# An encoder block with a 32-expert mixture on one core: a ring of eleven weight slots in place of ten, with a gather that reads the tokens themselves

## The chip, the core and the metric

The kernel runs on one core of one Trainium2 chip. The metric is device time in microseconds (us), smaller is better. The engines named below are TensorE (PE, with its weight loads PEld), VectorE (DVE), ScalarE (ACT), GpSimd (POOL) and SyncE (SP, which here issues nearly all transfers).

## The reference

One layer over 256 tokens of width 1024, all in 4-byte floats. Cut to what matters:

```
h = x
h = h + mixer(rmsnorm(h))                   # in-projection, dilated attention and MLA, out-projection
h = h + cross_attention(rmsnorm(h), rmsnorm(mem))   # 4 heads, 256 memory tokens
xt = rmsnorm(h) * g_moe                     # (256, 1024)
top_val, top_idx = top_k(xt @ w_router + b_router, 4)       # of 32 experts
gates = softmax(top_val)
for each expert e, for the tokens routed to it:
    gate, up = split(xt[tok] @ w_gate_up[e] + b_gate_up[e])  # (1024 x 2048)
    gate, up = min(gate, 7), clip(up, -7, 7)
    y[tok] += gates * (((up + 1) * gate * sigmoid(1.702 * gate)) @ w_down[e] + b_down[e])
return rmsnorm(h + y) * g_final
```

Each expert has 8 MB of gate-up weights and 4 MB of down weights, 384 MB in all.

## The kernel before

**Stages.** The in-projection z runs first (L1115: for each of eight row blocks k of `w_in`, eight matmuls into eight banks). Then come the attention parts, the cross-attention, its out-projection (`memory_out`, L1387), the router (L1400), the ranks of the tokens within their experts (L1419 to L1424), and the expert loop. The order on every engine is written out by hand. Semaphores join the engines.

**Items.** An expert's tokens are worked in blocks of 64. A block is an *item*; an expert with more than 64 tokens has two or more. An item is on PE: the biases (L1451), gate-up (`item`, L1467, 32 matmuls that the profile counts as 64), the gather of the *next* item's tokens (L1432), the scatter of the *previous* item's output into banks 4 to 7 (L1441), four transposes of the hidden rows (L1479), down (L1487, 16 matmuls, 32 in the profile), and two transposes of the scatter matrix (L1493). DVE clamps gate and up (L1070, L1071), joins them (L1074, L1077) and copies the gathered columns to `xgT` with the gain (`gathered_out`, L989); ACT does the sigmoid (L615) and the copies from PSUM (L618, L622, L624). Gate-up and gathering write two halves of 64 partitions of a bank by turns.

**The gather.** The normalised tokens are split in three bf16 parts (`part`, by `high_part`, `middle_left`, `middle_part`, `low_part` on ACT, DVE and one on POOL at L645), whose sum is the 4-byte value. 48 bf16 matmuls with the one-hot `pick` give the gathered columns.

**The ring.** Expert weights pass through `ring`, NSLOT slots of 2 MB. Expert e is six chunks j = 6e .. 6e+5, four of gate-up and two of down. SP loads chunk j when chunk j - NSLOT has been used by the expert's last item (`chunks_used`). Experts 7 to 26 are loaded in a loop by pairs of chunks (L374, 4 MB, which need two free slots and give notice once); the others one by one (L366). The first ten chunks are loaded ahead as their places come free (`load_chunk`, L327), since the same memory serves the attention parts:

```
            load_chunk(7)
            sp.wait_ge(S["wm_mm"], 4)
            load_chunk(8)
            load_chunk(9)
            sp.wait_ge(S["rt_mm"], 2)
            load_chunk(6)
```

`wm_mm` counts the four groups of `memory_out`, `rt_mm` the two router products.

**The end.** After the last scatter (`y_done`) DVE adds the banks to h (L1083), ACT squares the rows (L628), a small chain gives the scale (L663 to L674), DVE scales the rows (L1090), and SP writes two halves of 512 KB (L400).

Of the kernel before, what the change touches and what calls it, by code (L numbers as in the profile page):

```python
# [28 lines left out]
NSLOT = 10  # L29
REGION = (2, 3, 4, 5, 8, 9, 6, 7, 0, 1)  # L30
LEAD = 2
GROUP = 5
EPS = 1e-6
NORMS = ("x", "mem", "z", "o", "h", "f")
# [12 lines left out]
C_LOGM = C_ID + P  # L47
C_UP = C_LOGM + TT * SEQ
# [9 lines left out]
G_END = 43  # L58


def shape_constants():

    c = np.zeros((P, C_END), np.float32)
    p = np.arange(P)
    c[:, C_ID:C_ID + P] = np.eye(P)
    for t in range(TT):

        off = np.arange(SEQ)[None, :] - (t * P + p)[:, None]
        n = sum(((off % d == 0) & (np.abs(off) <= w // 2)).astype(int) for w, d in PATTERNS)
        c[:, C_LOGM + t * SEQ:C_LOGM + (t + 1) * SEQ] = np.where(n > 0, np.log(np.maximum(n, 1)), -1e30)  # L70
# [7 lines left out]
    return c  # L78


def encoder_kernel(nc, x, xT, mem, pos, pos_col, posk, consts, gains, w_in, w_q_b, w_kv_b, rel_cur, rel_prev, w_o,
# [9 lines left out]
    with ctx:  # L91
# [8 lines left out]
        work = sb("work", 2048 + 4096 + 2048 + 3072 + KC * NE)  # L100
        cst = sb("cst", C_END)
        gain = sb("gain", G_END)
# [9 lines left out]
        def col_area(lo, n):  # L112
            return work[:, lo:lo + n]

        def pair_area(lo, n):
            return work[:, 2048 + lo:2048 + lo + n]

        def turn_area(lo, n):
            return work[:, 6144 + lo:6144 + lo + n]

        def prob_area(lo, n):
            return work[:, 8192 + lo:8192 + lo + n]
# [4 lines left out]
        def slot(j):  # L127
            return region(REGION[j % NSLOT], 0, SLOT)

        def slot_pair(j):  # L130
            return ring[:, REGION[j % NSLOT] * SLOT:(REGION[j % NSLOT] + 2) * SLOT]

        def paired(e):
            return LEAD + GROUP <= e < NE - GROUP

# [13 lines left out]
        win = spl(ring[:, 0:KC * ZW], KC)  # L149
        z = spl(region(0, 0, TT * ZW), TT)  # L150
        bias = region(1, 0, TT * HEADS * SEQ).rearrange("p (t h k) -> p t h k", t=TT, h=HEADS)
        qb = spl(region(2, 0, TT * HEADS * DQB), TT)
        k96 = spl(region(2, 1536, TT * HEADS * DQB), TT)
        v_b = spl(region(2, 3072, TT * WA), TT)
        wmo = spl(ring[:, 0:KC * D], KC)


        def wmkv(k):
            return region((4, 5, 8, 9)[k // 2], k % 2 * 2 * D, 2 * D)
        wo = spl(ring[:, 4 * SLOT:4 * SLOT + KC * D], KC)  # L160
        wmq = spl(ring[:, 8 * SLOT:8 * SLOT + KC * D], KC)


        kT_flat = region(6, 0, KC * SEQ)
        kT_mem = spl(kT_flat, KC)
        v_mem = spl(region(6, 2048, TT * D), TT)
# [3 lines left out]
        wqb = spl(region(7, 0, 2 * HEADS * DQB), 2)  # L170
        wkvb = region(7, 1536, HEADS * (NOPE + DH))
        znT = spl(region(7, 2560, 3 * SEQ), 3)
        rope_t = region(7, 3328, 4 * HEADS * ROPE // 2)
        square_s = spl(region(7, 2560, 2 * SEQ), 2)
        square_sum = spl(region(7, 3072, 2 * SEQ), 2)
        qT_m = spl(region(7, 0, KC * SEQ), KC)
        bgu_raw = region(7, 2048, 2 * D)
# [8 lines left out]
        zero_bf = o_s.bitcast(bf16)  # L186
# [4 lines left out]
        steps = [a.bitcast(bf16).rearrange("p (k q) -> p k q", q=SEQ) for a in (pair_area(0, 4096), region(3, 0, 4096))]  # L191
        qT96 = spl(pair_area(0, HEADS * SEQ), HEADS)
        kT96 = spl(pair_area(2048, HEADS * SEQ), HEADS)
        rest = spl(pair_area(0, TT * D), TT)
        gate_s, up_s, sig_s, h_s = (pair_area(512 * i, 512) for i in range(4))
# [11 lines left out]
        pick = spl(turn_area(1664, TT * BLK // 2).bitcast(bf16), TT)  # L207
# [7 lines left out]
        probT = region(7, 0, 2048).rearrange("p (j g m q) -> p j g m q", j=2, g=2, m=TT)  # L215
# [3 lines left out]
        part = [spl(prob_area(i * D, D).bitcast(bf16), TT) for i in range(3)]  # L219
# [1363 lines left out]
```

## Time and profile before

| what | value |
|---|---|
| median of three runs | 1221.64 us (1220.99 to 1222.2) |
| the profiled execution | 1219.65 us |
| its span, first to last instruction | 1217.8 us |
| PE busy | 1140.9 us (94%) |
| DVE, ACT, POOL busy | 301.4, 199.2, 7.5 us |
| moved by DMA | 440.43 MB, mean 362 GB/s |
| PE share of the chain that ended last | 66%, DMA 19%, DVE 9% |
| items | 33 (L1070 ran 33 times) |

The span begins with the first instruction and ends with the last. The profiled execution takes 1.85 us beyond its span. Busy time says how long an engine had work, not what it cost the whole. The chain that ended last is followed back from the last instruction to what released each step.

### The profile page before, as it was taken

Reading aid. Unit: us, or ns where it says so; the run is one execution under the profiler, and the core shown is the slowest. Engines: PE = TensorE matmul, PEld = TensorE weight load, DVE = VectorE, ACT = ScalarE, POOL = GpSimd, SP = SyncE. Lnnn points to the kernel's source line nnn. Section 1 sums busy time; section 2 is a strip of 40 time slices with the busy share of each in tenths; the row PEclk is TensorE's granted clock in tenths of the full one; section 3 lists DMA queues with packets and bytes.
Section 4 is the critical chain, followed back from the end, with each engine's and each line's share of the span. In section 5 each row is a group of like instructions: output and inputs, shape, how many; then the busy total and the mean of one; then the engine's idle time right before and its main releaser. Section 6 shows DMA issues by size and latency. Waiting matters only on the chain.

```text
span 1217.8 us, 16578 instructions
## 1 busy us (share of the span) xinstructions
PE 1140.9 (94%) x6563; PEld 490.7 (40%) x6563; DVE 301.4 (25%) x683; ACT 199.2 (16%) x375; POOL 7.5 (1%) x13
## 2 busy tenths in 40 slices
PE   7999999998999999999988989889999999999995
PEld 3476555854333333333333333333333333333332
DVE  3366553148212111111211111111111121111113
ACT  2120551223111111111110111111111111111111
POOL 0000010000000000000000000000000000000000
PEclk9999999998999999999999999999999999999998
DMA  9800269326999999999999999999999999999993
GB/s 364 347 1 1 73 275 356 129 100 248 429 426 427 428 428 434 430 429 433 433 431 430 431 430 431 430 429 429 382 430 429 430 432 431 426 427 428 427 427 164
DMA packets 28572, 440.43 MB, mean 362 GB/s; under 512 B 4576, under 2 KB 4704, under 8 KB 10496
## 3 DMA queue, kind: packets, MB, share of 16 engines
q1 hardware_dynamic: 27504, 439.30, 85.3%
q8 instruction: 52, 0.85, 0.3%
q10 hardware_dynamic: 1008, 0.21, 0.1%
q14 instruction: 8, 0.07, 0.0%
HBM read 438.45 MB, written 1.05 MB: 361 GB/s over the span
## 4 chain that ended last, share of the span: by engine, by line
PE 66%; DMA 19%; DVE 9%; ACT 2%; issue 2%; DVEq 2%; SPq 0%; ACTq 0%
PE quad L1467 26%; DMA ring<-in_w_gate_up 19%; PE quad L1487 16%; PE quad L1115 2%; PE bank L1331 2%; PE bank L1115 2%; DVE work L1074 2%; DVE work L1070 2%; PE quad L1479 1%; PE bank L1137 1%; DVE work L1071 1%; ACT work L618 1%; PE bank L1207 1%; PE bank L1278 1%; PE quad L1286 1%
## 5 line engine op out<-in xcount | busy, mean ns | idle before, releaser
L1467 PE MATMUL quad<-ring,work 128*64 128x512 f32 x2112 | 465.8, 598 | 17.0 <-DMA ring<-in_w_gate_up 17.0
L1467 PEld LDWEIGHTS quad<-ring,work 128*64 128x64 f32 x2112 | 148.7, 138 | 315.5 <-issue 283.7
L1487 PE MATMUL quad<-ring,work 128*64 128x512 f32 x1056 | 233.9, 595 | 22.6 <-ACT work L618 22.6
L1487 PEld LDWEIGHTS quad<-ring,work 128*64 128x64 f32 x1056 | 72.8, 137 | 162.5 <-issue 132.0
L1070 DVE TENSOR_SCALAR work<-quad 128x512 f32<-128x512 f32 x33 | 22.8, 691 | 322.3 <-PE quad L1467 322.3
L615 ACT ACTIVATE work<-work 128x512 f32<-128x512 f32 x33 | 20.8, 630 | 464.0 <-DVE work L1070 464.0
L984 DVE CAST work<-cst 96x64 bf16 (+1 forms) x34 | 6.5, 191 | 335.3 <-PE quad L1467 335.3
L1441 PE MATMUL bank<-work 64*128 64x512 f32 x272 | 67.6, 615 | 0.7 <-ACT work L624 0.7
L1432 PEld LDWEIGHTS quad<-work 128*128 128x128 bf16 x1632 | 50.6, 99 | 29.1 <-issue 28.3
L622 ACT ACTIVATE work<-quad 128x512 f32<-128x512 f32 x33 | 19.7, 597 | 237.2 <-PE quad L1487 237.2
L1432 PE MATMUL quad<-work 128*128 128x64 bf16 x1632 | 54.6, 195 | 1.5 <-DVE work L960 1.5
L615 ACT ACT_TABLE_LOAD x33 | 42.3, 1283 | 1.1 <-issue 0.5
L1115 PE MATMUL quad<-ring,work 128*128 128x488 f32 x64 | 29.8, 612 | 8.1 <-DMA ring<-in_w_in 8.1
L618 ACT ACTIVATE work<-quad 128x512 f32<-128x512 f32 x33 | 19.7, 597 | 94.9 <-PE quad L1479 94.9
L979 DVE TENSOR_SCALAR work<-cst,work 128x64 bf16 (+1 forms) x68 | 14.2, 251 | 75.3 <-issue 75.2
L1441 PEld LDWEIGHTS bank<-work 64*128 64x128 f32 x272 | 23.5, 186 | 18.6 <-issue 16.0
L1331 PE MATMUL bank<-work,ring 128*128 128x256 f32 x128 | 27.9, 380 | 1.3 <-DVE work L679 1.3
L1115 PE MATMUL bank<-ring,work 128*128 128x488 f32 x64 | 27.5, 572 | 0.0
L1479 PEld LDWEIGHTS quad<-cst,work 128*128 128x128 f32 x132 | 13.8, 140 | 33.0 <-DVE work L989 33.0
L1479 PE MATMUL quad<-cst,work 128*128 128x128 f32 x132 | 21.7, 286 | 5.7 <-DVE work L989 5.7
L1331 PEld LDWEIGHTS bank<-work,ring 128*128 128x128 f32 x128 | 24.2, 190 | 4.8 <-DVE work L679 1.5
L1074 DVE SCALAR_TENSOR_TENSOR work<-work 128x512 f32<-128x512 f32 x33 | 22.8, 692 | 3.5
(260 smaller groups left out, 772.2 us busy)
## 6 DMA issues: line engine op xcount, KB each, us to landing
ring<-in_w_gate_up SPq DMA_DIRECT2D x40, 4096.0 KB, 35.1
ring<-in_w_gate_up SPq DMA_DIRECT2D x48, 2048.0 KB, 20.4
ring<-in_w_down SPq DMA_DIRECT2D x20, 4096.0 KB, 33.4
ring<-in_w_down SPq DMA_DIRECT2D x24, 2048.0 KB, 21.3
ring<-in_w_mkv SPq DMA_DIRECT2D x8, 1024.0 KB, 23.5
ring<-in_w_in SPq DMA_DIRECT2D x8, 976.0 KB, 16.7
ring<-in_w_o SPq DMA_DIRECT2D x1, 4096.0 KB, 12.9
ring<-in_w_mq SPq DMA_DIRECT2D x1, 4096.0 KB, 22.6
```

Of the source, the lines that this page charges most:

```text
L615: act.activation(sig_s, gate_s, ACT.Sigmoid, scale=ALPHA).then_inc(S["sig_ready"], 1)
L618: act.activation(hT, bank[2][:, :], ACT.Copy).then_inc(S["hid_ready"], 1)
L622: act.activation(o_s, bank[3][:, :], ACT.Copy).then_inc(S["out_copied"], 1)
L1070: dve.tensor_scalar(gate_s, bank[0][:, :], LIMIT, None, ALU.min).then_inc(S["gate_ready"], 1)
L1074: dve.scalar_tensor_tensor(up_s, up_s, 1.0, gate_s, ALU.add, ALU.mult).then_inc(S["gu_ready"], 1)
L1115: ins = mm(bank[4 * t + n][:, 0:ZN], nT[:, k, t * P:(t + 1) * P], win[:, k, n * ZN:(n + 1) * ZN], start=(k == 0), stop=(k == KC - 1))
L1331: ins = mm(bank[4 + c // 2][:, c % 2 * SEQ:(c % 2 + 1) * SEQ], wmq[:, k, c * P:(c + 1) * P], hT_s[:, k, :], start=(k == 0), stop=(k == KC ...
L1432: ins = mm(bank[2][:, c * BLK:(c + 1) * BLK], part[j][:, t, c * P:(c + 1) * P], pick[:, t, :], start=(j == 0 and t == 0), stop=(j == 2 and ...
L1441: ins = mm(bank[4 + 2 * t + n][:, :], gsel[lo:lo + BLK, t * P:(t + 1) * P], o_s[lo:lo + BLK, :], start=False, stop=last, skip_group_check= ...
L1467: ins = mm(bank[n // 2][lo:lo + BLK, :], xgT[:, k * BLK:(k + 1) * BLK], up_rows(j, k)[:, n * 512:(n + 1) * 512], start=False, stop=(k == K ...
L1479: ins = pe.transpose(bank[2][:, c * P:(c + 1) * P], h_s[:, c * P:(c + 1) * P], ident)
L1487: ins = mm(bank[3][n * BLK:(n + 1) * BLK, :], lhs, down_rows(j, f)[:, n * 512:(n + 1) * 512], start=(f == 0), stop=(f == KC - 1))
```

## The change

- The ring has eleven slots. Slot j is region j mod 11; the attention parts move to other regions. To make room, `work` loses its 3072-column score area, which now lies in region 7, and consts and gains shrink. The SP loop is written out; pairs are used for experts 7 to 26 where both chunks lie side by side.
- The chunks loaded ahead are 0 to 10, with other conditions for 6 to 10.
- The gather multiplies the 4-byte tokens h by a 4-byte `pick` that carries the norm's scale: four matmuls to rows of 64 tokens. ACT copies them (`xg_s`), PE transposes them, DVE adds the gain. The bf16 parts are gone on ACT, DVE and POOL.
- Banks 4 to 7 are opened with h (`residual_in`) in place of zeros.
- The last norm reads those banks; the output goes out in four pieces, one of them multiplied by POOL.
- The first loads are small (gains and one column block in one transfer, then half of `w_in`'s first block), and twelve bf16 matmuls on zeros (`warm`) stand ahead of the in-projection. ACT issues its small loads after the first has landed.

```diff
-NSLOT = 10
-REGION = (2, 3, 4, 5, 8, 9, 6, 7, 0, 1)
+NSLOT = 11
+PAIRED = range(7, 27)
...
+        def pair_first(j):
+            return j // NCH in PAIRED and j % 2 == 0 and j % NSLOT < NSLOT - 1
...
+            sp.dma_start(work[:, FRONT - G_END:FRONT + SEQ], xT[:, 0:G_END + SEQ]).then_inc(S["ld_first"], 16)
+            sp.dma_start(win(0, 0, half_row), w_in[0:P, 0:half_row]).then_inc(ld_win[0], 16)
+            sp.dma_start(win(0, half_row, ZW - half_row), w_in[0:P, half_row:ZW]).then_inc(S["ld_half"], 16)
...
             sp.wait_ge(S["bgu_ready"], 1)
+            load_chunk(6)
+            sp.wait_ge(S["om_mm"], MH)
             load_chunk(7)
             sp.wait_ge(S["wm_mm"], 4)
             load_chunk(8)
+            sp.wait_ge(S["wm_mm"], 5)
             load_chunk(9)
             sp.wait_ge(S["rt_mm"], 2)
-            load_chunk(6)
+            load_chunk(10)
...
-            memory_out(3, range(0, 4))
+            memory_out(3, range(0, 4)).then_inc(S["wm_mm"], 1)
...
             def gather():
-                for c in range(KC):
-                    for j in range(3):
-                        for t in range(TT):
-                            ins = mm(bank[2][:, c * BLK:(c + 1) * BLK], part[j][:, t, c * P:(c + 1) * P], pick[:, t, :],
-                                     start=(j == 0 and t == 0), stop=(j == 2 and t == TT - 1))
+                for t in range(TT):
+                    for n in range(2):
+                        ins = mm(bank[2][n * BLK:(n + 1) * BLK, :], pick[:, t, :], h[:, t, n * 512:(n + 1) * 512],
+                                 start=(t == 0), stop=(t == TT - 1))
...
+            def residual_in(t):
+                for n in range(2):
+                    mm(bank[4 + 2 * t + n][:, :], ident, h[:, t, n * 512:(n + 1) * 512], start=True, stop=False,
+                       skip_group_check=True)
...
+            def gathered_columns(w):
+                pe.wait_ge(S["xg_copied"], w + 1)
+                for c in range(4):
+                    ins = pe.transpose(bank[3][:, c * P:(c + 1) * P], xg_s[:, c * P:(c + 1) * P], ident)
+                ins.then_inc(S["xgT_mm"], 1)
...
                 scatter().then_inc(S["scattered"], 1)
-                pe.wait_ge(S["xg_ready"], w + 2)
+                gathered_columns(w + 1)
                 pe.wait_ge(S["hmid_ready"], w + 1)
                 for c in range(4):
                     ins = pe.transpose(bank[2][:, c * P:(c + 1) * P], h_s[:, c * P:(c + 1) * P], ident)
                 ins.then_inc(S["hid_mm"], 1)
                 pe.wait_ge(S["hid_ready"], w + 1)
+                pe.wait_ge(S["xg_ready"], w + 2)
...
+            pe.wait_ge(S["warm_ready"], 1)
+            for i in range(12):
+                mm(bank[7][:, :], warm[:, 0:P], warm[:, :], start=True, stop=True)
...
-            for j in range(4):
-                t, n = divmod(j, 2)
-                dve.tensor_tensor(h[:, t, n * 512:(n + 1) * 512], bank[4 + j][:, :], h[:, t, n * 512:(n + 1) * 512],
-                                  ALU.add).then_inc(S["f_ready"], 1)
+            link(dve.tensor_copy(h[:, 0, 512:D], bank[5][:, :]))
+            link(dve.tensor_tensor_reduce(spare[:, 512:D], h[:, 0, 512:D], bank[5][:, :], 1.0 / D, 0.0, ALU.mult, ALU.add,
+                                          ss[:, 1:2]))
...
+            out_scaled(1, 0)
+            out_scaled(1, 1)
+            out_scaled(0, 0)
```

On PE, one item of the expert loop stood so before (`quad` is banks 0 to 3, `bank` the others; the counts are of matmuls written, two records each in the profile where the operands are 4 bytes wide and not a transpose):

```order
L1451 MATMUL quad<-work 64x512 x4
L1467 MATMUL quad<-ring,work 64x512 x32
L1472 REGISTER_ALU
L1432 MATMUL quad<-work 128x64 x48
L1441 MATMUL bank<-work 128x512 x4
L1479 MATMUL quad<-cst,work 128x128 x4
L1487 MATMUL quad<-ring,work 64x512 x16
L1493 MATMUL quad<-cst,work 128x128 x2
```

And now (`y_banks` is banks 4 to 7):

```order
L1467 MATMUL quad<-work 64x512 x4
L1481 MATMUL quad<-ring,work 64x512 x32
L1486 REGISTER_ALU
L1441 MATMUL quad<-h,work 64x512 x4
L1457 MATMUL y_banks<-work 128x512 x4
L1449 MATMUL quad<-cst,work 128x128 x4
L1493 MATMUL quad<-cst,work 128x128 x4
L1502 MATMUL quad<-ring,work 64x512 x16
L1508 MATMUL quad<-cst,work 128x128 x2
```

The 48 gather matmuls became four, and four transposes (L1449) came in between the scatter and the transposes of the hidden rows.

On PE, between the router's last product and the first item, before:

```order
L1400 MATMUL quad<-work,ring 128x32 x4
L1419 MATMUL quad<-work,up_bf 128x32
L1421 MATMUL quad<-work,ones_bf 128x32
L1422 MATMUL quad<-work,up_bf 128x32
L1423 MATMUL quad<-work,ones_bf 128x32
L1424 MATMUL quad<-work,ones_bf 128x32
L1502 MATMUL bank<-work 128x512 x4
L1432 MATMUL quad<-work 128x64 x48
L1509 MATMUL quad<-cst,work 32x128 x2
```

And now:

```order
L1403 MATMUL quad<-work,ring 128x32 x4
L1423 MATMUL y_banks<-h,cst 128x512 x2
L1429 MATMUL quad<-work,up_bf 128x32
L1431 MATMUL quad<-work,ones_bf 128x32
L1432 MATMUL quad<-work,up_bf 128x32
L1433 MATMUL quad<-work,ones_bf 128x32
L1434 MATMUL quad<-work,ones_bf 128x32
L1423 MATMUL y_banks<-h,cst 128x512 x2
L1441 MATMUL quad<-h,work 64x512 x4
L1519 TENSOR_LOAD work
L1519 ISA x2
L1449 MATMUL quad<-cst,work 128x128 x4
```

The four bf16 matmuls on zeros (L1502) gave way to four 4-byte ones that bring in h (L1423), two ahead of the ranks and two behind; the first gather is followed by a trip over ACT to the transposes at L1449.

## Rows read from the trace of the kernel before

**Rows 1.** The page: the span, and what DMA moved in 40 equal slices.

```profile
span 1217.8 us, 16578 instructions
...
GB/s 364 347 1 1 73 275 356 129 100 248 429 426 427 428 428 434 430 429 433 433 431 430 431 430 431 430 429 429 382 430 429 430 432 431 426 427 428 427 427 164
```

**Rows 2.** Stretches of the expert loop: each engine's busy time, clock, DMA share, GB/s.

```profile
320.00:563.00 243.00, 235.34 (x1474) 87.20 (x1470) 40.35 (x90) 30.58 (x46) 0.00 (x0) 1.00 1.01 430
563.00:834.00 271.00, 246.62 (x1496) 89.59 (x1494) 41.14 (x93) 32.45 (x48) 0.00 (x0) 0.98 1.00 431
```

**Rows 3.** The chain that ended last: start, us, what.

```profile
403.69 13.76 PE quad L1467 x64
...
430.37 13.76 PE quad L1467 x64
...
793.83 40.20 DMA ring<-in_w_gate_up
834.08 7.11 PE quad L1467 x32
...
854.10 13.76 PE quad L1467 x64
...
1188.33 3.68 PE quad L1467 x16
...
1205.06 2.00 PE bank L1441 x8
```

**Rows 4.** SP's transfers in order of time: start, us over which they were issued.

```profile
812.68 12.33 SPq L374 DMA_DIRECT2D ring<-in_w_gate_up  x2
861.15 0.33 SPq L374 DMA_DIRECT2D ring<-in_w_down  x1
```

**Rows 5.** Timeline of one item, from the end of gate-up to down.

```profile
390.69 1.57 PE L1432 MATMUL quad<-work 128*128 128x64 bf16 x48
...
392.19 1.99 PE L1441 MATMUL bank<-work 64*128 64x512 f32 x8
...
394.35 0.66 PE L1479 MATMUL quad<-cst,work 128*128 128x128 f32 x4 [0.17 <-DVE work L989]
...
395.69 7.09 PE L1487 MATMUL quad<-ring,work 128*64 128x512 f32 x32 [0.69 <-ACT work L618]
```

**Rows 6.** Timeline of the first matmuls.

```profile
8.10 5.79 PE L1115 MATMUL quad<-ring,work 128*128 128x488 f32 x8 [8.10 <-DMA ring<-in_w_in]
...
13.73 3.44 PE L1115 MATMUL bank<-ring,work 128*128 128x488 f32 x8
```

**Rows 7.** Timeline from the router to the first item, with one stretch's busy times.

```profile
273.09 1.04 PE L1394 MATMUL quad<-cst,h 128*128 128x128 f32 x8
...
279.54 3.68 PE L1387 MATMUL bank<-ring,work 128*128 128x512 f32 x8
...
281.15 2.12 POOL L645 TENSOR_TENSOR work<-work 128x1024 bf16<-128x1024 f32 x1 [98.68 <-ACT work L586]
281.44 1.87 DVE L973 CAST work<-work 128x32 bf16<-128x32 f32 x1
...
283.88 0.69 DVE L933 TENSOR_TENSOR h<-bank,h 128x512 f32<-128x512 f32 x1
...
289.11 0.18 PE L1424 MATMUL quad<-work,ones_bf 128*128 128x32 bf16 x1
...
290.00:292.00 2.00, 1.10 (x3) 0.15 (x1) 1.97 (x8) 1.95 (x3) 0.00 (x0) 0.50 0.98 414
...
296.51 13.90 PE L1467 MATMUL quad<-ring,work 128*64 128x512 f32 x64
```

**Rows 8.** Timeline of the end, behind the last scatter.

```profile
1208.40 1.06 ACT L628 ACTIVATE work<-h 128x1024 f32<-128x1024 f32 x1 [1.98 <-DVE h L1083]
...
1210.78 0.17 DVE L663 TENSOR_SCALAR stat<-stat 128x2 f32<-128x2 f32 x1 [1.22 <-ACT work L628]
...
1213.52 1.54 SPq L400 DMA_DIRECT2D out<-h  x2
```

More of the change, by code:

```diff
@@ L46 @@
 C_ID = 0
-C_LOGM = C_ID + P
-C_UP = C_LOGM + TT * SEQ
+C_UP = C_ID + P
 C_IOTA = C_UP + P
@@ L127, in slot, with pair_second, loads_before @@
         def slot(j):
-            return region(REGION[j % NSLOT], 0, SLOT)
+            return region(j % NSLOT, 0, SLOT)
         def slot_pair(j):
-            return ring[:, REGION[j % NSLOT] * SLOT:(REGION[j % NSLOT] + 2) * SLOT]
-        def paired(e):
-            return LEAD + GROUP <= e < NE - GROUP
+            return region(j % NSLOT, 0, 2 * SLOT)
+        def pair_first(j):
+            return j // NCH in PAIRED and j % 2 == 0 and j % NSLOT < NSLOT - 1
+        def pair_second(j):
+            return j % 2 == 1 and pair_first(j - 1)
+        def loads_before(j):
+            return sum(not pair_second(i) for i in range(j % NSLOT, j, NSLOT))
         def up_rows(j, k):
@@ L404, in _ @@
+            sp.wait_ge(S["st_out"], 16 * 4)
         @block.scalar
         def _(act):
-            act.dma_start(gain[:, :], gains).then_inc(S["ld_gain"], 16)
+            act.wait_ge(S["ld_first"], 16)
             act.dma_start(poscol_i[:, :], pos_col).then_inc(S["ld_small"], 16)
@@ L986, in gathered_out @@
             def gathered_out(w):
-                dve.wait_ge(S["gathered"], w + 1)
-                dve.tensor_tensor(spl(xgT, KC), spl(bank[2][:, :], KC),
-                                  over(gain[:, G_MOE:G_MOE + KC].unsqueeze(2), [P, KC, BLK]), ALU.mult).then_inc(S["xg_ready"], 1)
+                dve.wait_ge(S["xgT_mm"], w + 1)
+                halves = gain[:, G_MOE:G_MOE + KC].rearrange("p (n c) -> p c n", n=2)
+                dve.tensor_tensor(xgT.rearrange("p (c n s) -> p c n s", c=4, n=2),
+                                  bank[3][:, :].rearrange("p (c n s) -> p c n s", c=4, n=2),
+                                  over(halves.unsqueeze(3), [P, 4, 2, BLK]), ALU.mult).then_inc(S["xg_ready"], 1)
             residual(0)
@@ L1453, in chunk_in @@
             def chunk_in(j):
-                if paired(j // NCH):
-                    j -= j % 2
-                loads = [i for i in range(j % NSLOT, j + 1, NSLOT) if j % 2 == 0 or not paired(i // NCH)]
-                pe.wait_ge(ld_slot[j % NSLOT], 16 * len(loads))
+                if pair_second(j):
+                    j -= 1
+                pe.wait_ge(ld_slot[j % NSLOT], 16 * (loads_before(j) + 1))
             def item(w, j):
@@ L1534, in _ @@
             pe.wait_ge(S["gsel_ready"], items + 1)
-            scatter(last=True).then_inc(S["y_done"], 1)
+            for t in range(TT):
+                scatter((t,), last=True).then_inc(S["y_done"], 1)
 def kernel(x, mem, positions, g_mix, w_in, g_q_a, w_q_b, g_kv_a, w_kv_b, rel_bias, g_out_a, g_out_b, w_o,
```

352 lines of the change are left out of this document (167 added, 185 removed).

## The prediction, made before the result was known

> **What bounds the kernel now.** I read the page first. DMA moves 426 to 434 GB/s in nearly every slice from the eleventh on [rows 1], so the expert loop is held by its weights as much as by PE. The stretches say the same [rows 2]: 430 and 431 GB/s at a DMA share of 1.0, while PE is busy 235.3 of 243 us in the first and only 246.6 of 271 us in the second. So PE does not wait early in the loop and does wait later.
>
> The two rates are close. The chain shows the gate-up of consecutive items 26.68 us apart where nothing waits (403.69 to 430.37) [rows 3]. An expert's 12.58 MB at 430 GB/s are 29.26 us. Each expert therefore eats 2.6 us of the lead that the ten slots give, until PE stands at the end of a transfer. One expert has two items (33 items, 32 experts). SP's list shows where: its pairs come 48.5 us apart between 812.68 and 861.15 instead of some 27 [rows 4], because the slots are kept for the second item. The chain has a DMA wait up to 834.08 in the first item of that expert, and the second item's gate-up starts at 854.10 [rows 3]. This second item hands DMA a whole item's time, and after it the chain has no DMA wait until 1188.33, which is in the last expert, on its last gate-up chunk. By PE's pace alone that item's gate-up would have begun at 854.10 + 12 x 26.68 + 3.6 (the down biases) = 1177.9 and its fourth quarter at 1188.2. So that last wait is worth only 0.2 us.
>
> The end is thus a sum of two bounds: DMA up to 834.08 (counted from the moment the first used slots are given back), then PE for the rest of that item and 13 more. A change of DMA counts in the first part, a change of an item on PE in the second alone. The expert's number is 19 if the loads are counted off.
>
> **The start.** PE's first eight records take 5.79 us, the next eight 3.44 with the last one's drain, and later starts are 3.27 apart; from 8.10 to 13.73 is 5.63, so 2.36 us are lost to slow first matmuls [rows 6]. The twelve matmuls on zeros need no load and can run while the first transfers are under way. Before, 1.52 MB (half of xT, the first block of w_in) stood ahead of the first matmul; now it is 0.65 MB. The other 0.87 MB at 364 GB/s (first slice, [rows 1]) are 2.4 us. The in-projection is worked by PE without a gap behind it, so both pass on: 4.7 us. Bounds: 2.4 (the zeros do not help) to 5.2.
>
> **Entry to the experts.** DVE's cast at L973 took 1.87 us for 32 columns while POOL's subtraction ran from 281.15 to 283.27; then the residual came at 283.88 [rows 7], though PE's memory_out (279.54 + 3.68) was done at 283.22, before the cast. Without the parts and without POOL, DVE waits for PE, and everything behind comes 0.6 us sooner. The Trainium skill (SBUF — State Buffer, section on SBUF's two separate sides) says that VectorE and GpSimd share one pair of ports as an exclusive lock; the row agrees.
>
> residual_in(1) lies in PE's wait for the second mask and costs nothing (its 1.72 us fit a gap of about 2; if they did not, up to 0.3). residual_in(0) is two 4-byte matmuls of 512 columns over the whole array, 0.86 us each by 2 x 0.43 (the L1467 records are two abreast, 13.76/64 = 0.215), so 1.7 in place of the zeros' 1.9. The low parts no longer hold the gather. Behind residual_in(0): gather 1.7, ACT's copy and its waits 0.8, transposes 0.7, DVE's copy with gain 0.8, biases 0.5. The ranks ended at 289.3 (L1424) and now end 0.6 sooner, 288.7; + 1.7 + 1.7 + 0.8 + 0.7 + 0.8 + 0.5 = 294.9, against 296.51 [rows 7]. Gain 1.6 us, so the first item starts 6.3 us sooner in all. The chunks 6 to 10 are ordered sooner or no later, none on the path.
>
> **The slot.** With eleven slots, chunk j is ordered one chunk earlier, and the number of transfers between the first freed slot and any given chunk falls by one: 2.097 MB at 430 GB/s is 4.9 us. This holds only where PE has come to wait again before expert 19. Over the lead of ten slots PE first waited in about the eleventh item. Now an item costs a little more (next part), 26.9; the lead is larger by 4.9, and 29.26 - 26.9 = 2.36 is eaten at each. (11 x 2.58 + 4.9) / 2.36 = 14 items, still well before 19. So all 4.9 count. SP's written-out loop orders the same transfers; with four or five in flight its few more instructions hide. Unpaired chunks at the ring's seam can only let PE start sooner.
>
> **An item on PE.** Between the end of gate-up and down lie now [rows 5]: the gather, 390.69 to 392.19, 1.50; the scatter, from 392.19, some 1.75 without drain; a wait for DVE of 0.17; the transposes at 394.35; ACT's copy; down at 395.69.
> - The new gather: four matmuls of 512 columns in 4 bytes, 64 rows each to two halves of a bank, as L1467 does: 8 x 0.215 = 1.72, so +0.22.
> - Scatter as before: 392.41 to 394.16.
> - The new transposes: eight take 1.04 with drain at L1394 [rows 7], so 0.11 each: 0.43. Their input, ACT's copy, starts after the gather and lasts 0.6, until about 393.3: hidden behind the scatter.
> - Hidden transposes at 394.6 in place of 394.35: +0.25. The wait for DVE is gone; it pays a part. ACT's copy follows, and down starts 0.25 later. DVE's gained copy, 0.69 as for L933 [rows 7], after the new transposes (394.85), ends at 395.6, just before down would start at 395.94; if late, it would add its lateness to each item.
> Sum: +0.23 us per item. From below 0 (drains smaller than I take), from above 0.46 (the scatter's whole 1.99 counted). It counts for the rest of item 19 and 13 more: 14 x 0.23 = 3.2 us. In the 19 before, it only shortens waits. The ACT table load of each item stays in ACT's idle time. Fewer PE instructions cost nothing now and save nothing.
>
> **The end.** From the scatter at 1205.06 to the span's end are 12.7 us. ACT now squares banks directly: a 1024-column square is 1.06 [rows 8], with its read 1.25, so the mean stands at about 1207.1 + 1.45 = 1208.55 in place of 1210.78: 2.2 us. The scale chain is as long. Then four transfers, where two took 1.54 to issue [rows 8]; half of the last row block goes over ACT (0.6) and POOL (half of 2.12 in [rows 7], 1.1). The last piece is ready near 1212.4 and is issued behind three others, until some 1213.9, against 1213.52 + 1.54 = 1215.06; it is also half as long. I take 1.7 us of gain; bounds 1.0 and 2.5. [...]
>
> **Sum.** 4.7 + 1.6 + 4.9 - 3.2 + 0.2 (the last DMA wait) + 1.7 = 9.9 us. The profiled execution, 1219.65, becomes 1209.7. It lay 2.0 us below the median of the three runs, so on their scale the forecast is 1221.64 - 9.9 = 1211.7.
>
> **Rivals.**
> - *The clock falls at the entry.* The stretch 290 to 292 has a granted clock of 0.50 [rows 7], the 1.2 GHz level, after the gaps that PE had around the router. If it falls again, residual_in(0), the gather and the transposes double: 1.7 + 1.7 + 0.2 = 3.6 us, which DMA's start takes on in full: 1215.3. For it: those gaps remain. Against: residual_in(1) fills nearly 2 us of them. The Trainium skill (TensorE: Matmul & The Clock Gate, "What's actually happening") says that the clock follows how busy the array has been, which leaves both open. 30 in 100.
> - *The item grows more than by its matmuls.* If down must wait for ACT's second copy or DVE's late one, for 0.8 us per item instead of 0.23, PE hardly waits for DMA at all and nearly each item counts: (0.8 - 0.23) x 14 = 8 us back, 1219.7, no change that can be told. For it: a trip PE to ACT to PE to DVE to PE is new in each item. Against: all but 0.3 us of it is covered above. 6 in 100.
> - *Slower.* The gather's halves do not run abreast: 3.44 instead of 1.72, the item 28.6 us. Then PE bounds the loop alone, 33 x 1.95 = 64 us more work against the 24.4 us that PE was idle from 563 to 834 [rows 2] and the gains; with the first item at 290.2 the last scatter starts at 290.2 + 33 x 28.6 + 3.6 = 1237.6, and the run takes about 1252. The point from which it decides: with the other gains the loop breaks even at about 1.0 us per item. Against: L1467 has the same shapes and halves. 3 in 100, and 2 for other slower ways.
> - *The slot brings nothing* (PE never waits before expert 19): 4.9 us less, 1216.6. Against: the count of 14 items. 4 in 100.
> - *Better:* item unchanged, start at its upper bound: 1211.7 - 3.2 - 0.5 - 0.8 = 1207.2. 10 in 100.
> - The forecast itself, 1209.5 to 1214: 45 in 100.
>
> **Range and chances.** 1206 to 1218 holds forecast, better case, clock case and the slot's, and leaves out the last two ways. A difference of 0.2% (2.4 us) is about what a measurement of this kernel can tell. Faster by over that: 0.89; within: 0.06; slower: 0.05.
>
> **What would show it.** Right: first in-projection records near 5.8 us and eight in 3.3 from the first; first gate-up near 290; items 26.9 apart; DMA waits from about the fourteenth item; a wait in the first item of expert 19 near 823; last scatter near 1197, the span near 1208. Wrong: items over 27.2 apart; waits of PE at the new transposes or at down for DVE; a clock of 0.5 between the ranks and the first item; a last gate-up that still waits for DMA, which would mean that DMA gained less than PE.

## The result, and the profile after

| | before | after |
|---|---|---|
| median | 1221.64 us (1220.92 to 1225.86, 5 runs) | 1214.24 us (1213.99 to 1215.7, 5 runs) |
| span of the profiled execution | 1217.8 us | 1212.5 us |
| last scatter begins | 1205.06 | 1201.76 |

The ratio is 0.9933, with a 95% interval of 0.9915 to 0.995: faster by 7.4 us. The two profiled executions differ by 5.3 us in span, since that of before lay 2.0 us under its median and that of after on it.

The page of after, beside [rows 1]: PE is busy 96% of the span in place of 94%, and DMA's slices read much as before.

```profile
span 1212.5 us, 13954 instructions
...
PE 1162.4 (96%) x5355; PEld 477.2 (39%) x5355; DVE 301.7 (25%) x681; ACT 214.8 (18%) x404; POOL 6.6 (1%) x13
...
GB/s 361 354 1 1 126 274 328 139 139 295 430 426 429 426 431 431 427 436 432 430 430 431 429 427 437 431 432 416 409 431 425 436 432 432 422 428 426 429 425 83
```

The chain that ended last, beside [rows 3]: start, us, what.

```profile
54.88 3.29 PE y_banks L1118 x8
...
781.16 42.52 DMA ring<-in_w_gate_up
823.73 8.78 PE quad L1481 x32
...
845.87 13.73 PE quad L1481 x64
...
1201.76 2.00 PE y_banks L1457 x8
```

The last in-projection group starts at 54.88; before, it started at 59.72. The wait in expert 19 ends at 823.73 in place of 834.08. So by there the kernel is 10.35 us ahead, and at the last scatter 3.3. The way from the one to the other took 370.98 us before and takes 378.03 now. Part of that is in the second row: the 32 records behind the wait last 8.78 us, where [rows 3] has 7.11 for the same work.

The timeline of the first matmuls, beside [rows 6]:

```profile
1.19 4.59 PE L1109 MATMUL y_banks<-ring 128*128 128x512 bf16 x12 [1.19 <-DVE ring L691]
5.61 0.98 PE L1118 MATMUL quad<-ring,work 128*128 128x488 f32 x2
```

The timeline of the entry, beside [rows 7] (start, us, what; in brackets how long the engine was idle before, and what released it), and one stretch's busy times (the granted clock is the third number from the end):

```profile
280.67 1.29 PE L1403 MATMUL quad<-work,ring 128*128 128x32 f32 x8 [0.78 <-DVE ring L680]
...
281.77 3.46 PE L1423 MATMUL y_banks<-h,cst 128*128 128x512 f32 x4
...
283.60 0.18 DVE L965 CAST work<-work 128x32 bf16<-128x32 f32 x1
...
285.07 0.18 PE L1429 MATMUL quad<-work,up_bf 128*128 128x32 bf16 x1
...
285.20 1.96 PE L1423 MATMUL y_banks<-h,cst 128*128 128x512 f32 x4
...
287.09 1.94 PE L1441 MATMUL quad<-h,work 128*64 128x512 f32 x8
...
291.79 1.91 PE L1481 MATMUL quad<-ring,work 128*64 128x512 f32 x8
...
282.00:285.00 3.00, 3.00 (x4) 1.07 (x5) 1.80 (x9) 1.11 (x7) 0.00 (x0) 0.53 1.01 431
```

Both masks were ready at 283.8 (the cast at L965 is the last step), but the ranks' matmuls start at 285.07: residual_in(1) took 3.46 us ahead of them, twice what residual_in(0) takes at 285.20. The stretch shows a granted clock of 0.53, near the 1.2 GHz level, behind PE's gap of 0.78 us and two router products of 32 columns. The first gate-up product starts 4.72 us sooner than before, and 4.84 of that came with the in-projection.

The timeline of one item, beside [rows 5]:

```profile
551.14 1.99 PE L1457 MATMUL y_banks<-work 64*128 64x512 f32 x8
551.27 0.60 ACT L594 ACTIVATE work<-quad 128x512 f32<-128x512 f32 x1 [0.36 <-PE quad L1441]
...
553.06 0.66 PE L1449 MATMUL quad<-cst,work 128*128 128x128 f32 x4
553.55 0.60 PE L1493 MATMUL quad<-cst,work 128*128 128x128 f32 x4
553.75 0.69 DVE L982 TENSOR_TENSOR work<-quad,work 128x512 f32<-128x512 f32 x1 [1.33 <-PE quad L1449]
...
554.84 2.37 PE L1502 MATMUL quad<-ring,work 128*64 128x512 f32 x10 [0.69 <-ACT work L613]
```

Nothing waits there but down for ACT's copy (0.69, as before). Items are 27.08 us apart (845.87 above, the next at 872.95).

The end, beside [rows 8]:

```profile
1203.79 1.02 ACT L626 ACTIVATE work<-y_banks 128x1024 f32<-128x1024 f32 x1
...
1206.41 2.06 DVE L1072 SCALAR_TENSOR_TENSOR h<-y_banks,stat,work 128x512 f32<-128x512 f32 x3
...
1207.18 2.78 SPq L406 DMA_DIRECT2D out<-h  x4
1207.36 1.27 POOL L649 TENSOR_TENSOR h<-h,work 128x512 f32<-128x512 f32 x1 [928.15 <-ACT h L630]
```

From the last scatter to the end are 10.74 us in place of 12.74.

### The profile page after: what moved, and what is told of

The parts are those of the page before. It is cut to its first block, busy times and chain, and to the rows that moved or that the text cites. A ratio compares the mean times of both kernels' runs of the same rounds, so it can differ in the third digit from the quotient of the medians.

```text
span 1212.5 us, 13954 instructions
## 1 busy us (share of the span) xinstructions
PE 1162.4 (96%) x5355; PEld 477.2 (39%) x5355; DVE 301.7 (25%) x681; ACT 214.8 (18%) x404; POOL 6.6 (1%) x13
## 4 chain that ended last, share of the span: by engine, by line
PE 85%; DMA 10%; ACT 2%; DVE 1%; issue 0%; POOLq 0%; ACTq 0%
PE quad L1481 32%; PE quad L1502 17%; DMA ring<-in_w_gate_up 10%; PE y_banks L1457 5%; PE quad L1441 4%; PE y_banks L1334 2%; PE y_banks L1118 2%; PE quad L1118 2%; PE quad L1449 2%; ACT work L613 2%; PE y_banks L1140 1%; PE quad L1467 1%; PE y_banks L1210 1%; PE y_banks L1281 1%; PE quad L1289 1%; PE quad L1390 1%
## 5 line engine op out<-in xcount | busy, mean ns | idle before, releaser
L1502 PE MATMUL quad<-ring,work 128*64 128x512 f32 x1056 | 233.9, 595 | 22.7 <-ACT work L613 22.7
L1502 PEld LDWEIGHTS quad<-ring,work 128*64 128x64 f32 x1056 | 72.9, 137 | 162.4 <-issue 131.9
L1457 PE MATMUL y_banks<-work 64*128 64x512 f32 x272 | 67.6, 615 | 0.7 <-ACT work L619 0.7
L1441 PE MATMUL quad<-h,work 128*64 128x512 f32 x272 | 64.1, 593 | 0.0
L971 DVE TENSOR_SCALAR work<-cst,work,stat 128x64 f32 (+1 forms) x68 | 18.2, 311 | 90.9 <-issue 90.9
L1457 PEld LDWEIGHTS y_banks<-work 64*128 64x128 f32 x272 | 23.5, 186 | 43.6 <-issue 42.7
L982 DVE TENSOR_TENSOR work<-quad,work 128x512 f32<-128x512 f32 x34 | 23.5, 691 | 46.1 <-PE quad L1449 46.1
L1441 PEld LDWEIGHTS quad<-h,work 128*64 128x64 f32 x272 | 19.1, 137 | 39.4 <-issue 38.0
L1334 PE MATMUL y_banks<-work,ring 128*128 128x256 f32 x128 | 27.9, 380 | 1.3 <-DVE work L680 1.3
L1118 PE MATMUL y_banks<-ring,work 128*128 128x488 f32 x64 | 28.0, 572 | 0.0
L1334 PEld LDWEIGHTS y_banks<-work,ring 128*128 128x128 f32 x128 | 24.3, 190 | 4.8 <-DVE work L680 1.5
L1449 PEld LDWEIGHTS quad<-cst,work 128*128 128x128 f32 x136 | 14.2, 140 | 26.6 <-issue 25.0
```

The source lines that it names most:

```text
L982: dve.tensor_tensor(xgT.rearrange("p (c n s) -> p c n s", c=4, n=2), bank[3][:, :].rearrange("p (c n s) -> p c n s", c=4, n=2), over(halve ...
L1118: ins = mm(bank[4 * t + n][:, 0:ZN], nT[:, k, t * P:(t + 1) * P], win(k, n * ZN, ZN), start=(k == 0), stop=(k == KC - 1))
L1334: ins = mm(bank[4 + c // 2][:, c % 2 * SEQ:(c % 2 + 1) * SEQ], wmq[:, k, c * P:(c + 1) * P], hT_s[:, k, :], start=(k == 0), stop=(k == KC ...
L1441: ins = mm(bank[2][n * BLK:(n + 1) * BLK, :], pick[:, t, :], h[:, t, n * 512:(n + 1) * 512], start=(t == 0), stop=(t == TT - 1))
L1449: ins = pe.transpose(bank[3][:, c * P:(c + 1) * P], xg_s[:, c * P:(c + 1) * P], ident)
L1457: ins = mm(bank[4 + 2 * t + n][:, :], gsel[lo:lo + BLK, t * P:(t + 1) * P], o_s[lo:lo + BLK, :], start=False, stop=last, skip_group_check= ...
```

## The experiments

All were timed in five rounds beside the kernel before; ratios are to that one, with 95% intervals. "The distance" below is the time from the wait's end in expert 19 to the last scatter.

### e1_ten_slots: ten slots again, the rest as changed

```diff
-NSLOT = 11
+NSLOT = 10
+NREG = 11
-        ring = sb("ring", NSLOT * SLOT)
+        ring = sb("ring", NREG * SLOT)
...
-            sp.wait_ge(S["rt_mm"], 2)
-            load_chunk(10)
```

> The changed kernel with ten slots in use (the eleventh region stays for the attention parts, no chunk is loaded ahead into it). Theory of two bounds: DMA sets the time until the stall in the first item of expert 19, so one slot less moves that stall 4.9 us later (2.097 MB at 430 GB/s) and the rest follows: about 1219.1 us beside 1214.2, last scatter near 1206.7 in place of 1201.76, and PE meets its first DMA wait about two items earlier than the fifteenth item. Rival, the slot is only slack: PE's pace alone sets the end, 1214 us, and DMA waits stay few. Rival, DMA-bound to the very end: also 4.9 us, but with a long DMA wait in the last expert.

1217.0 us, ratio 0.9979 [0.9965, 0.9992]; its seven runs lie in two groups, four of 1216.5 to 1217.0 and three of 1220.8 to 1221.05 us. The chain:

```profile
291.76 13.73 PE quad L1480 x64
...
790.52 37.26 DMA ring<-in_w_gate_up
827.82 7.09 PE quad L1480 x32
```

Expert 19's wait ends 4.1 us later than after's. Counted from the first gate-up group of the same execution it is 536.06 us in place of 531.75 (823.73 - 291.98 in after). The slot is worth 4.3 us there, and 4.5 to 4.7 against e5, e7, e9 and e10 below, whose distances from first group to wait are 531.32 to 531.54; 4.9 were foreseen. PE waits seven times for DMA, 11.5 us in all, where after has five waits and 7.6 us; the first (until 651.86 in place of 705.52) comes two items sooner, as expected. The last scatters of the two profiled executions (1204.16 and 1201.76) are only 2.4 us apart, since behind the wait this one needs 7.09 us where after's has 8.78. The edit also changes the pairs: with ten slots all chunks of experts 7 to 26 go in pairs, where eleven slots leave one pair in eleven apart, so e1 changes a little more than the slot.

### e2_columns_hidden: the gathered columns' transposes go behind those of the hidden rows

```diff
-                gathered_columns(w + 1)
+                pe.wait_ge(S["xg_copied"], w + 2)
                 pe.wait_ge(S["hmid_ready"], w + 1)
...
                 ins.then_inc(S["hid_mm"], 1)
+                gathered_columns(w + 1)
                 pe.wait_ge(S["hid_ready"], w + 1)
-                pe.wait_ge(S["xg_ready"], w + 2)
```

(The columns also go to bank 0 in place of bank 3.)

> The gathered rows are transposed behind the transposes of the hidden rows, into bank 0, while ACT copies the hidden rows, and down no longer waits for the gained copy. Theory of two bounds: an item falls from 27.09 to about 26.60 us (the 0.49 us from L1449 to L1493), which counts in the 14 items from the stall on and not in the 19 before: 14 x 0.49 = 6.9 us, about 1207.4 us; the DMA waits before expert 19 grow by as much as the items shrink. Rival, every item counts: 33 x 0.49 = 16 us, 1198 us. Rival, the cost of an item is not in these transposes but in a wait for ACT or DVE: the item stays near 27.1 us and the time at 1214 us.

1206.88 us (1204.5 to 1211.22), ratio 0.9886 [0.9868, 0.9904]. The chain:

```profile
823.70 7.09 PE quad L1481 x32
...
1193.93 2.00 PE y_banks L1457 x8
```

The transposes now run while ACT copies the hidden rows. Items are 26.65 us apart, 0.44 less, and expert 19's wait ends where it did, though 19 items ahead of it are shorter. PE's waits for DMA grew instead: 13.5 us in seven, where after has 7.6 in five. The distance fell from 378.03 to 370.23: 1.69 for the slow records of after, and 6.11, which is 14 x 0.44 within 0.1. So 14 items count, not 33.

### e3_unpaired and e4_hidden_unpaired: every chunk by itself, without and with e2's edit

```diff
-PAIRED = range(7, 27)
+PAIRED = range(0)
```

> Every chunk is loaded by a transfer of its own, none by pairs. Theory: the stall in expert 19 is a wait for the pair of its gate-up chunks 2 and 3, behind which PE still has both to work (7.09 us for 32 records). Alone, chunk 2 would be done when chunk 3 lands, so one chunk's work, about 3.4 us, leaves the path: about 1210.8 us. Rival, transfers of 2 MB move less per second than those of 4 MB: at 429 in place of 431 GB/s the 106 chunks before it come about 2.4 us later, and the gain is 1 us or none. Rival, pairs do not matter: 1214.2 us.

> Both edits of e2 and e3. If they simply added, 10.3 us: 1203.9 us. The theory of two bounds says less: in the changed kernel the last gate-up chunk is needed at about 1184.8 and lands near 1177.5, so only some 7.5 us can be taken from PE before the end waits for DMA again. Then the chain ends with a DMA wait in the last expert, and the time is about 1206.5 us (7.3 from that slack, with 3.4 us of chunk 3 always left behind its landing).

1212.0 us, ratio 0.9922 [0.9908, 0.9935], and 1209.29 us, ratio 0.9898 [0.9883, 0.9913]. The chain of the first, then of the second:

```profile
780.38 46.19 DMA ring<-in_w_gate_up
826.61 3.65 PE quad L1481 x16
```

```profile
1134.45 45.19 DMA ring<-in_w_gate_up
1179.68 3.65 PE quad L1481 x16
```

Alone, unpairing lets PE start one quarter earlier than the pair did and wait only for the last, which lands 2.9 us later than the pair did, with 3.4 less work behind it. That is a gain of 0.6 us; the other 1.7 of the 2.3 between its last scatter (1199.51) and that of after (1201.76) are the slow 8.78 us of after, which this execution hasn't. With e2's shorter items DMA catches PE again in the last expert and the gains don't add: the last scatter comes at 1196.39, 2.5 us behind that of e2 alone, though the intervals of the two ratios overlap. From 320 to 815 us DMA moved 428 GB/s with every transfer of 2 MB (both kernels) and 430 with pairs of 4 MB (after and e2).

### e5_no_warm and e6_big_first: the start without the zeros' matmuls, and with the old first loads

```diff
-            for i in range(12):
+            for i in range(0):
```

```diff
-            sp.dma_start(win(0, 0, half_row), w_in[0:P, 0:half_row]).then_inc(ld_win[0], 16)
-            sp.dma_start(win(0, half_row, ZW - half_row), w_in[0:P, half_row:ZW]).then_inc(S["ld_half"], 16)
+            sp.dma_start(win(0), w_in[0:P, :]).then_inc(ld_win[0], 16)
```

(The second also loads half of xT at once, as before.)

> The twelve matmuls on zeros are left out. Theory: the first records of the in-projection go at half speed again, as before (5.63 us for the first eight in place of 3.28), and the 2.4 us pass on in full to the first item, to the stall in expert 19 and to the end: about 1216.6 us beside 1214.2, the first gate-up near 294.2. Rival: the in-projection has slack behind it (loads of later blocks, VectorE) and the time stays at 1214.2.

> The first loads are large again: gains with half of xT in one transfer, and w_in's first block in one. The twelve matmuls on zeros stay. Theory: the first product starts near 8.1 in place of 5.61, 2.4 to 2.5 us later, and passes on in full: about 1216.7 us. Rival: with the first block complete sooner than its second half was, nothing is waited for later and part of it comes back: 1215.5 us or less.

1217.73 us (1213.69 to 1218.25), ratio 0.9961 [0.9947, 0.9974], and 1215.5 us, ratio 0.9946 [0.9932, 0.9959]. The first matmuls of e5, then of e6:

```profile
5.12 1.97 PE L1118 MATMUL quad<-ring,work 128*128 128x488 f32 x2 [5.12 <-DMA ring<-in_w_in]
```

```profile
6.86 1.06 PE L1113 MATMUL quad<-ring,work 128*128 128x488 f32 x2 [1.35 <-DMA ring<-in_w_in]
```

In e5 the load has landed at 5.12, and the product runs at half speed. The last in-projection group starts at 56.19, which is 1.31 later than in after, where I had 2.4. The other profiles show why: the warm-up outlasts the load. In e9 (below) all twelve zeros' matmuls took 0.43 us each and held the first product until 6.17, a full us past the landing in e5. Against the in-projection's last start in the profiles of the kernels that have both warm-up and small loads (54.38 in e7 to 55.97 in e4) the warm-up saves 0.2 to 1.8 us. With the old loads the first product waits for them until 6.86, and the last in-projection group starts 1.32 later than in after. I had expected 8.1, its start in the kernel before, and 2.4 to 2.5 us. So the smaller transfers bring 1.25 of the 2.49 us by which after's first product comes sooner. The other 1.24 are not theirs; e6 still differs from before in that ACT issues its small loads later, from 4.39 in place of 0.71 us on, and no run isolates that.

But the profiled execution of e5 took only 1213.69 us. Its entry had no fall of the clock, so its first gate-up group starts at 291.86, 0.12 before that of after (291.98), despite the later start. Nor had e6's: both have PE's gap of 0.78 us and a clock of 1.00 in the stretches from 280 to 288. Two runs of e5 took 1213.69 and 1214.46 us, the other three 1217.7 to 1218.25. A single execution tells nothing of 1.3 us here.

### e7_no_residual and e8_ranks_first: what stands in the gap of the entry

e7 opens banks 6 and 7 with a short bf16 product in place of residual_in(1) and so leaves the residual of tokens 128 to 255 out of the output. e8 is e2 with residual_in(1) behind the first gather.

```diff
-            residual_in(1)
             pe.wait_ge(S["ones_ready"], 1)
+            for n in range(2):
+                mm(bank[6 + n][:, :], up_bf[0:96, :], bgu[0:96, n * 512:(n + 1) * 512], start=True, stop=False,
+                   skip_group_check=True)
             pe.wait_ge(S["mask_ready"], 1)
```

> This leaves out the residual of tokens 128 to 255: banks 6 and 7 are opened by two bf16 matmuls on other data, in place of the 4-byte ones on h. Theory: in the changed kernel those ran at a granted clock of 0.53, took 3.46 us and held the ranks until 285.07, though the second mask was there at 283.88. Without them the ranks start near 283.9, the first item near 290.6 in place of 291.79, and the time is about 1213.0 us. If the clock falls a little later instead, on residual_in(0) or the gather, the 1.2 us are lost there again: 1214.2. Rival, the masks or picks set the start anyway: 1214.2 with the first gate-up at 291.8.

> The edit of e2 (gathered rows transposed behind the hidden ones, pairs kept), and residual_in(1) put behind the first gather instead of ahead of the ranks. Theory: the ranks start with the second mask, 1.2 us sooner, residual_in(0) covers the wait for the picks, and residual_in(1) runs while ACT copies the gathered rows, which it delays by about 0.8 us: the first item starts some 0.4 us sooner, 1206.5 us beside e2's 1206.9. If the clock falls on the gather or either residual_in, up to 1.7 us are lost: 1208.5.

1216.47 us (1212.06 to 1217.71), ratio 0.9958 [0.9944, 0.9971], and 1211.67 us, ratio 0.9913 [0.9898, 0.9928]. The timelines of PE, e7 first:

```profile
283.16 0.19 PE L1433 MATMUL quad<-work,ones_bf 128*128 128x32 bf16 x1 [1.44 <-DVE work L965]
...
283.27 3.25 PE L1423 MATMUL y_banks<-h,cst 128*128 128x512 f32 x4
286.45 2.30 PE L1443 MATMUL quad<-h,work 128*64 128x512 f32 x8
```

```profile
284.07 3.76 PE L1423 MATMUL y_banks<-h,cst 128*128 128x512 f32 x4
287.77 2.44 PE L1440 MATMUL quad<-h,work 128*64 128x512 f32 x8
```

In both the ranks come sooner (283.16 and 283.95), since nothing is ahead of them. And in both the clock falls on what comes next, residual_in(0) and the gather. From the last in-projection group to the first gate-up product e7 takes 237.13 us and e8 238.79, after 236.91 and e2 236.90. What was gained ahead of the ranks did not last to the end of the entry. In e8 the stretch 282 to 284 has PE busy 0.13 of 2 us at a clock of 0.50, and it stays at that level until past 287. Not all of e8's 1.9 us is the clock's: residual_in(1) now takes 1.82 us between the gather and the transposes, where PE otherwise waits 0.70 for ACT's copy. The medians lie 2.2 us above after's and 4.8 above e2's; e8's profile has one more fall, behind the down biases (below), and for e7, whose profiled execution was its fastest, the profile does not explain the median.

### e9_after_again, e10_filler and e11_hidden_filler: the gap filled

e9 is the changed kernel once more. In e10 three bf16 matmuls of no use into the free bank 3 stand in PE's 0.78 us wait. e11 is e2 with the same lines.

```diff
             columns(1, 1)
+            for i in range(3):
+                mm(bank[3][0:P, :], up_bf[0:96, :], bgu[0:96, 0:512], start=True, stop=True)
             router(1, 1).then_inc(S["rt_mm"], 1)
```

> The changed kernel itself, as the anchor of this group. Both theories: about 1214 us, a ratio of 0.993 to the kernel before. By the theory that drops of the granted clock make the spread of its times, an execution whose mean granted clock is higher by 0.002 to 0.003 is shorter by 2 to 4 us, and in an execution without a drop at the entry of expert 0 the first gate-up product starts before 291.7 us.

> Three matmuls of no use fill TensorE's 0.78 us wait before the second router product, with all results as before. Theory A (TensorE's low activity at the entry of expert 0 makes the clock fall on the residual product): the clock stays at full speed, residual_in(1) takes 1.96 and not 3.46 us, the ranks product ends at about 283.9 and the first gate-up product starts at about 290.6, 1.2 us earlier; about 1213.0 us, ratio 0.992. Theory B (the fall is set by something longer than this gap and only moves): a fall still shows between 280 and 292 us, the first gate-up product starts at 291.7 or later, and the time is 1214 to 1216 us.

> The kernel of e2_columns_hidden with the three filler matmuls of e10_filler. Theory A: 1.2 us below e2_columns_hidden's 1206.9, about 1205.7 us, ratio 0.9875, with the first gate-up product at about 291.0 in place of 292.23. Theory B: 1206.9 us or more, with the clock fall in another place of the entry.

1214.52 us (two runs of 1212.15 and 1212.26, four of 1214.5 to 1215.07), ratio 0.9929 [0.9908, 0.995]; 1211.79 us (1211.02 to 1212.68), ratio 0.9913 [0.9894, 0.9932]; 1206.96 us, ratio 0.9868 [0.9845, 0.989]. The timelines of PE at the entry, e9 and then e10:

```profile
281.23 1.08 PE L1403 MATMUL quad<-work,ring 128*128 128x32 f32 x8 [0.79 <-DVE ring L680]
282.15 3.40 PE L1423 MATMUL y_banks<-h,cst 128*128 128x512 f32 x4
...
292.30 1.05 PE L1481 MATMUL quad<-ring,work 128*64 128x512 f32 x4
```

```profile
281.23 1.08 PE L1403 MATMUL quad<-work,ring 128*128 128x32 f32 x8
282.15 1.96 PE L1425 MATMUL y_banks<-h,cst 128*128 128x512 f32 x4
...
290.90 2.34 PE L1483 MATMUL quad<-ring,work 128*64 128x512 f32 x10
```

Both executions have the last router product at 281.23, and all between is the same work. With the gap filled residual_in(1) takes 1.96 us, and the first gate-up product starts 1.40 us sooner. That is the fall's price. The other profiles agree: from the last in-projection group to the first gate-up product it is 236.86 to 236.91 us in the five with the fall on residual_in(1) (after, e1, e2, e3, e9) and 235.46 to 235.48 in the six without (e4, e5, e6, e10, e11, e12).

That the filling prevents the fall is less sure. None of the three profiles with the filled gap has it, but of the eight with residual_in(1) behind an unfilled gap three (e4, e5, e6) have none either. The medians of e9 and e10 differ by 2.7 us, and the two intervals overlap. Of the 3.1 us between the last scatters of their profiled executions (1202.06 and 1198.97) 1.40 are the entry's and 1.69 another fall behind the down biases, which e9's had and e10's had not. In e11 the entry is as good (first product at 291.12 against 292.23 in e2), and yet the median is e2's. Its runs lie in two groups, 1204.4 to 1205.2 and 1208.7 to 1209.0 us. The profiled one is of the upper group, and its timeline shows another fall, right behind the down biases:

```profile
1082.02 4.20 PE L1537 MATMUL y_banks<-work 32*128 32x512 f32 x8
1086.15 1.07 PE L1469 MATMUL quad<-work 96*64 96x512 bf16 x4
1087.00 9.48 PE L1483 MATMUL quad<-ring,work 128*64 128x512 f32 x32
```

These eight matmuls use 32 of 128 rows. The stretch 1086 to 1090 has a clock of 0.50. This fall, too, comes in some executions only: in the profiles of e5, e6, e8, e9 and e11, for 1.7 or 3.3 us, and not in those of before, after, e1, e2, e3, e4, e7 and e10.

### e12_early_biases: e11 with the down biases ahead of expert 15

```diff
-                if e == NE - 4:
+                if e == 15:
                     down_biases()
```

> The kernel of e11_hidden_filler with the down biases (eight matmuls of 32 rows, 3.6 us on TensorE) ahead of expert 15 in place of expert 28. Theory of two bounds (DMA up to expert 19, TensorE behind it): their 3.6 us come out of TensorE's waits for DMA before expert 19 and cost nothing any more; the quarter of expert 19 that waits still starts near 822.8, and the first of the next 12 items' distances to hold them is gone, so the last scatter comes at least 3.6 us sooner. Theory that the clock falls behind them, since they use 32 of 128 rows: the drop at 1084 to 1092 is gone too, 2.9 us in that profile, though it may come back beside expert 15, where it is hidden. Together 1200.5 to 1203.5 us against e11_hidden_filler's 1206.96, the lower group of its runs (1204.5) less 3.6 being 1200.9. DMA ends at about 1183 and the last gate-up quarter has 6 to 7 us of slack, so a short DMA wait in the last expert may show. Rival (TensorE's time counts everywhere, or the drops just move): 1205 to 1207 us.

1204.13 us (1203.2 to 1205.01), ratio 0.9856 [0.9835, 0.9877]; the lowest median of all. The chain:

```profile
821.51 7.09 PE quad L1483 x32
...
1130.35 43.61 DMA ring<-in_w_gate_up
1174.00 3.65 PE quad L1483 x16
...
1190.71 2.00 PE y_banks L1459 x8
```

The timeline behind the biases in their new place:

```profile
698.12 15.18 PE L1483 MATMUL quad<-ring,work 128*64 128x512 f32 x64
```

The 3.6 us cost nothing ahead of expert 19: from the first gate-up product to the end of its wait it is 531.43 us, and 531.67 in e11. The clock falls behind the biases here as well (15.18 us in place of 13.9, and 0.66 in the stretch 696 to 700), but where PE waits for DMA later it costs nothing, and e12's four runs have no upper group as e11's had. But e12's runs are no shorter than e11's lower group (1204.4 to 1205.2) by anything that can be told, and the intervals of the two ratios overlap. The end is at a new limit: the last gate-up quarter waits for DMA until 1174.0, 2.4 us later than PE's pace from 821.51 would have had it. So the distance is 369.20, only 1.0 less than e2's. That I had given DMA 6 to 7 us of slack there, with "a short wait may show", is where my 1200.5 to 1203.5 was too low.

## Why the prediction was right, and where its sizes were off

The forecast was 1211.7 us and the result 1214.24. That is in the range, but just outside the 1209.5 to 1214 of the forecast itself and nearer to the clock rival's 1215.3. The mechanism of two bounds held; the sum was 2.5 us too large. The prediction's steps, one by one:

- **Two bounds, DMA to expert 19 and then PE for 14 items**: held. e2 changed 33 items and was paid for 14; e12 moved 3.6 us of PE work ahead of the border and it vanished.
- **Start, 4.7**: 4.84 in the profile (59.72 to 54.88). Of this 2.49 is the first product's earlier start (5.61 for 8.10), and the rest its full speed. That the first part hit its 2.4 is partly luck: e6 gives the smaller transfers, to which the prediction put all of it, only 1.25. And the two parts overlap: without the warm-up only 1.31 is lost, because the load had landed half a us before the warm-up let the first product go.
- **Slot, 4.9**: 4.3 to 4.7 by e1. The profiles of before and after have 5.63 in this part. Of this 1.3 stand between before and e1, and no run isolates them; the order of the early loads is a candidate that was not tried.
- **Item, +0.23**: +0.41 (27.09 in place of 26.68). The gather took the 1.72 foreseen. Two terms were too small: the scatter, "some 1.75 without drain", takes 1.92 on the chain, and the new transposes take 0.59 in place of 0.43. Against them, down starts 1.12 us after the start of the hidden transposes, where the prediction kept the 1.34 of [rows 5]; these transposes no longer stand behind a wait and take 0.45 on the chain in place of 0.67. The upper bound of 0.46 held the sum. Over 14 items +0.41 is 5.7, not 3.2, and 5.36 with 0.4 us of last DMA wait given back, which I had at 0.2. The first DMA wait came in the 16th item, not the 14th.
- **Entry, 1.6**: nothing came, -0.12. This is the step that failed. What came is the rival "the clock falls at the entry" with another victim: residual_in(1), of which the prediction said that it costs nothing in a gap of about 2 us. It took 3.46 and held the ranks for 1.2 us. Without the fall the way from the last in-projection group to the first gate-up is 235.46 to 235.48 us, and 236.79 before, so the entry itself is worth 1.3. The 236.79 hold a fall too (0.50 from 290 to 292 [rows 7]), which the forecast left out and gave to a rival. The Trainium skill (TensorE: Matmul & The Clock Gate, "What's actually happening") says that the clock follows how busy the array has been; e10, where the gap is filled and no fall comes, agrees; e4, e5 and e6, with the gap unfilled and no fall, show that the gap alone does not decide it. The rival's price, 3.6 us, was too high: 1.40 measured. None of its three pieces, residual_in(0), the gather and the transposes, ran slow in after (1.96, 1.94 and 0.66 us); residual_in(1) did.
- **A fall at the wait in expert 19**, 1.69 us in the profile of after, stood in no part of the forecast. It is the second one of that execution that cost time; one more, behind the DMA wait up to 755.32 (8.78 us as well), lies ahead of the border. In e9's profile it came behind the down biases instead, at the same price: the distances are 378.03 in both, and 376.34 in e10, e7 and e1, which have none there.
- **DVE's cast**: 0.18 us (L965) where it had taken 1.87 beside POOL's subtraction, as foreseen.
- **End, 1.7**: 2.0. DVE's three products, which read a bank each, took 0.69 each and 2.06 us in all while POOL's 1.27 us ran beside them, so POOL did not hold them up.

In the traces: 4.84 - 0.12 + 5.63 - 5.36 - 1.69 + 2.0 = 5.3 us, the difference of the spans. The forecast had 9.9. It lost 1.7 at the entry, 2.4 by the item (with the last DMA wait) and 1.7 by the fall in expert 19, and won 0.1 at the start, 0.7 in the DMA part and 0.3 at the end. The medians differ by 7.4, since the profiled execution of before was a short one.

What moves two executions of one kernel apart by 2 to 4 us is probably how many such falls lie where PE sets the end. The mean granted clock of the runs speaks for it: 0.994 to 0.995 in e1's shorter runs and 0.992 in its longer ones, 0.994 to 0.996 and 0.990 to 0.992 in e11's. But only one execution of each kernel has a profile, so this is not shown. In e10 all six runs lie within 1.7 us. What decides in a given execution whether a fall comes was not settled: e4, e5 and e6 had none at their entries, with the same gap.

## What to carry to other kernels

Find the last place where the engine that ends the run still waits for DMA. Work of that engine costs nothing ahead of it and its full price behind, so a step that can be placed freely (here the biases) belongs ahead, until DMA is the limit at the end too. A transpose that needs no result of the moment goes into the wait for another engine's copy; here that brought 6.1 us for a change of order. A short idle gap of TensorE before wide matmuls can cost more than its length (here 0.78 us idle, and in five of eight profiles 1.4 us behind it). It can be filled with real work or even with useless products; the three profiles with it filled had no fall, which speaks for it and doesn't prove it. And judge edits of 1 to 2 us by the profile's distances between marks, not by one time.

## What the hardware showed that I had not expected

- The clock falls to 1.2 GHz for stretches of about 3 to 7 us in a loop that is otherwise busy: behind a gap of 0.78 us and products of 32 columns, behind waits for DMA, and behind eight matmuls of 32 rows, each in some executions and not in others. It then stretched matmuls whose inputs were long ready (3.46 for 1.96 us).
- Twelve bf16 matmuls of 512 columns on zeros ran at 0.43 us each from 1.19 us on. In the twelve profiles that have them they took 4.09 to 5.30 us in all, as the last ones were faster or not, so that the first product stood behind them for up to 1.2 us.
- A 4-byte scatter of eight records with 64 rows in takes 1.92 us on the chain, a gather of eight with 64 columns out 1.72.
